# Moving eight row products and two table units of an expert layer ahead of its first pass

## The chip, the cores and the metric

The kernel runs on one core of a Trainium2 chip. Its engines are TensorE (matmuls), VectorE, ScalarE, GpSimd (here it mainly issues indirect DMAs) and SyncE (issues plain DMAs); 16 DMA engines move the data. The metric is the device time of one execution in microseconds (us), lower is better.

## The reference

One encoder block on 256 tokens of width 2048: two kinds of attention, an output projection, and then a product-key expert layer (PEER). The change touches only the last part:

```
qr = (h @ w_pq).reshape(b, t, 8, 2, 128)              # queries of 8 heads, two halves
sc = einsum(qr, sub_keys)                             # 128 scores per half
s_top, i_top = top_k(sc, 16)
cand = s_top[..., 0, :, None] + s_top[..., 1, None, :]
c_top, c_pos = top_k(cand, 16)                        # 16 picks per head
expert = i0 * 128 + i1                                # one of 16384 experts
g = softmax(c_top)
a = gelu(einsum(u_tab[expert], h))                    # 128 picks per token
out = einsum(g * a, v_tab[expert])
```

The tables `u_tab` and `v_tab` have 16384 rows of 2048 float32 numbers, 8 KB a row.

## The kernel before

The two halves of the tokens are treated in different ways, at the same time.

Tokens 128 to 255 are **dense**. TensorE reads each table in 128 units of 128 experts, 1 MB each. In the **first pass** (`u_chunk`) it multiplies unit after unit of `u_tab` with the tokens, 16 matmuls a unit; in the **second pass** (`v_chunk`) it multiplies the gated results with units of `v_tab`. Ring buffers hold the units: four in the first pass (`ring[0..3]`, two in the `raw` tile and two in `late`), six in the second. SyncE and ScalarE issue the loads of the first pass, each when the unit that held the buffer has been used. In the second pass GpSimd gathers the units from the seventh on, and leaves out the table rows of experts that no token uses.

Tokens 0 to 127 are **sparse**, one token per partition. For each of the 128 picks GpSimd gathers one table row per token (1 MB in all, an indirect DMA), and VectorE multiplies it with the token. The list `ROWS` has 256 of them: rows 0 to 127 are of `u_tab` ("u rows", one dot product each, `next_row`), rows 128 to 255 of `v_tab` ("v rows", added to the output in PSUM; rows whose weight is zero are not fetched). `BUF` tells in which of 8 buffers row r lands. Buffers 0 and 1 are free early. Buffers 2 to 5 are in the tile `late`, which holds the split activations and weights until the query projection ends. Buffers 6 and 7 lie over the scores and are used from row `R_MORE` on. GpSimd issues rows 0 to `ROWS_U` - 1, and after that one unit of `v_tab` and some rows in turn; `end` in that loop sets how many rows stand behind each unit. All waits of an engine are in program order, so a gather that waits for a buffer holds up everything behind it on GpSimd.

Ahead of the first pass stands the **query projection** (`wide_piece`, 64 pieces of `w_pq`, two to a loaded block). ScalarE makes the high part of a piece (`w_hi`), VectorE the low part (`w_lo`, `split_lo_half`, called by `weights_low`), and TensorE multiplies both. Four pieces can be in work (`NPART`), and four blocks can be loaded (`NRAW`); SyncE loads a block when the low parts of the block four earlier are made. VectorE puts the picks (`top_k`) of the first `N_AHEAD` heads between these low parts, and after the projection the picks of the rest, each with two rows:

```
for hp in range(N_AHEAD, NH):
    top_k(0, hp)
    row_numbers(hp)
    next_row(2)
for hp in range(NH):
    top_k(1, hp)
    next_row(2)
next_row(2)
```

I call one turn of these loops a **round**: there are 13 of them before. After them VectorE does four more rows, waits until ScalarE has taken the exponentials of the gates (`cexp_done`, in ScalarE's order behind the GELU of unit 60), and normalises the gates. Two rows later it copies the transposed picks (`slotT`), builds one-hot tables (`hots`), and from unit 64 on applies gates to the units (`gate`, `apply`), one row for each two units. `hs` is the normalised token that each u row is multiplied with; its gain vector lies in row buffer 1 until `hs` is made.

## Time and profile before

| what | value |
|---|---|
| median of 3 runs | 1543.37 us (1543.35 to 1543.79) |
| the profiled execution | 1542.8 us, span of its trace 1540.8 us |
| query projection, about | 408 to 508 us of the span |
| first pass (128 units of `u_tab`) | 509 to 1004 us |
| second pass (128 units of `v_tab`) | 1005 to 1538 us |
| busy share of the span | TensorE 95%, VectorE 75%, ScalarE 32%, GpSimd 28% |
| moved by DMA | 516 MB |
| granted TensorE clock, mean | 0.991 |

All times inside the kernel are read in us from the start of the span. The profile counts an engine as busy while an instruction runs on it, also while that instruction is held up inside. Of the DMA engines it gives the mean busy share and the rate.

### The profile page before, as it was taken

The page shows a single profiled execution, that of the slowest core. Times are in us where ns is not written, and L with a number is a line of the kernel's source. Part 1 is how long each engine was busy: PE and PEld are TensorE (multiplying, and loading weights), DVE is VectorE, ACT ScalarE, POOL GpSimd, SP SyncE. Part 2 cuts the span into 40 slices and gives each one's busy share as a digit, 9 for nine tenths or more (in the row PEclk, how much of TensorE's full clock was granted, in tenths as well). Part 3 has the DMA queues.
Part 4 walks back from the last instruction along what each step waited for, and adds up shares of the span by engine and source line. Part 5 has one row for each costly group of instructions (what it writes and reads, how often), then busy time and mean ns, then how long its engine had stood idle before and what let it go on. Part 6 is the DMA issues. An engine that isn't in the chain of part 4 may idle for free.

```text
span 1540.8 us, 21876 instructions
## 1 busy us (share of the span) xinstructions
PE 1457.5 (95%) x7977; PEld 1095.4 (71%) x7977; DVE 1155.3 (75%) x1797; ACT 488.4 (32%) x1402; POOL 429.7 (28%) x422
## 2 busy tenths in 40 slices
PE   8999999999999999999999999988778898999998
PEld 6767888888999999999999999943323333334333
DVE  5425688576777999992387777797766899999996
ACT  6647566765655100000254444472000000000000
POOL 2020000000000422230111111164454566666661
PEclk9999999999999999999999999999999999999999
DMA  9774544637574999999999999999999999999995
GB/s 352 264 138 122 161 124 137 218 124 255 196 253 168 375 422 421 422 421 422 418 421 422 422 410 405 419 413 417 419 418 418 406 390 390 405 405 384 399 402 225
DMA packets 115529, 516.24 MB, mean 335 GB/s; under 512 B 26113, under 2 KB 28289, under 8 KB 63313
## 3 DMA queue, kind: packets, MB, share of 16 engines
q0 software_dynamic: 57776, 294.93, 48.3%
q1 hardware_dynamic: 47744, 153.04, 27.7%
q10 hardware_dynamic: 9936, 67.40, 10.5%
q8 instruction: 34, 0.56, 0.1%
q14 instruction: 39, 0.31, 0.1%
HBM read 628.91 MB, written 3.41 MB: 410 GB/s over the span
## 4 chain that ended last, share of the span: by engine, by line
PE 51%; DMA 28%; DVE 12%; issue 4%; POOL 3%; ACT 1%; SPq 0%; POOLq 0%; DVEq 0%; ACTq 0%
PE ps L1572 18%; DMA late<-in_u_tab 11%; DVE ps L1183 9%; PE ps L1356 6%; PE ps L1361 6%; PE ps L1358 6%; DMA late<-in_v_tab,acts 6%; DMA raw<-in_v_tab,acts 3%; PE ps L1617 3%; DMA late<-in_u_rows,sel 3%; PE ps L1378 2%; PE ps L1520 2%; PE ps L1515 2%; PE ps L1516 2%; DMA raw<-in_u_tab 2%
## 5 line engine op out<-in xcount | busy, mean ns | idle before, releaser
L859 DVE TENSOR_TENSOR w_lo<-raw,w_hi 128x512 fp32r<-128x512 f32 (+1 forms) x288 | 188.8, 682 | 130.8 <-ACT w_hi L552 129.1
L1572 PE MATMUL ps<-acts,late 128*128 128x128 f32 x2048 | 240.4, 276 | 6.5 <-DMA late<-in_u_tab 5.7
L1572 PEld LDWEIGHTS ps<-acts,late 128*128 128x128 f32 x2048 | 233.1, 192 | 10.7 <-DMA late<-in_u_tab 7.8
L1572 PE MATMUL ps<-acts,raw 128*128 128x128 f32 x1984 | 232.2, 276 | 3.6 <-DMA raw<-in_u_tab 2.8
L1572 PEld LDWEIGHTS ps<-acts,raw 128*128 128x128 f32 x1984 | 225.8, 192 | 7.0 <-DMA raw<-in_u_tab 4.9
L552 ACT ACTIVATE w_hi<-raw 128x512 fp32r<-128x512 f32 (+1 forms) x288 | 170.1, 622 | 85.8 <-PE ps L1520 41.9
L1617 PE MATMUL ps<-raw,acts 128*128 128x512 f32 x352 | 163.0, 613 | 21.2 <-DMA raw<-in_v_tab,acts 19.8
L1617 PE MATMUL ps<-late,acts 128*128 128x512 f32 x336 | 155.6, 611 | 21.3 <-DMA late<-in_v_tab,acts 19.2
L1617 PE MATMUL ps<-acts 128*128 128x512 f32 x336 | 154.8, 609 | 22.0 <-DMA acts<-in_v_tab,acts 21.2
L508 POOL DMA_INDIRECT late<-in_u_rows,sel x70 | 85.8, 1225 | 271.4 <-DVE late L1174 260.7
L1183 DVE SCALAR_TENSOR_TENSOR ps<-late,sel,ps 128x2048 f32<-128x2048 f32 x63 | 148.3, 2355 | 12.2 <-DMA late<-in_v_tab,acts 5.2
L1183 DVE SCALAR_TENSOR_TENSOR ps<-acts,sel,ps 128x2048 f32<-128x2048 f32 x63 | 148.3, 2354 | 8.4 <-DMA acts<-in_v_tab,acts 1.8
L1356 PE MATMUL ps<-w_hi,hT_hi 128*128 128x512 f32 (+1 forms) x448 | 148.5, 412 | 2.9 <-DVE hT_lo L872 2.6
L1617 PEld LDWEIGHTS ps<-raw,acts 128*128 128x128 f32 x352 | 66.4, 194 | 115.3 <-issue 76.8
L508 POOL DMA_INDIRECT acts<-in_u_rows,sel x58 | 66.7, 1150 | 281.5 <-DVE acts L1174 178.1
L1617 PEld LDWEIGHTS ps<-late,acts 128*128 128x128 f32 x336 | 62.7, 193 | 112.9 <-issue 68.8
L1617 PEld LDWEIGHTS ps<-acts 128*128 128x128 f32 x336 | 63.1, 193 | 112.0 <-issue 71.6
L1361 PE MATMUL ps<-w_lo,hT_hi 128*128 128x512 f32 (+1 forms) x448 | 137.6, 388 | 0.6 <-DVE w_lo L859 0.6
L1358 PE MATMUL ps<-w_hi,hT_lo 128*128 128x512 f32 (+1 forms) x448 | 138.0, 389 | 0.0
L1356 PEld LDWEIGHTS ps<-w_hi,hT_hi 128*128 128x128 f32 x448 | 80.8, 189 | 24.0 <-issue 6.5
L1361 PEld LDWEIGHTS ps<-w_lo,hT_hi 128*128 128x128 f32 x448 | 84.4, 189 | 18.2 <-DVE w_lo L859 1.1
L1174 DVE SCALAR_TENSOR_TENSOR late<-late,acts 128x2048 f32<-128x2048 f32 x40 | 90.7, 2287 | 8.8 <-DMA late<-in_u_rows,sel 8.7
(225 smaller groups left out, 1938.4 us busy)
## 6 DMA issues: line engine op xcount, KB each, us to landing
raw<-in_w_in SPq DMA_DIRECT2D x72, 512.0 KB, 3.8
late<-in_u_tab SPq DMA_DIRECT2D x33, 1024.0 KB
raw<-in_u_tab SPq DMA_DIRECT2D x32, 1024.0 KB
late<-in_u_tab ACTq DMA_DIRECT2D x31, 1024.0 KB
raw<-in_u_tab ACTq DMA_DIRECT2D x30, 1024.0 KB
raw<-in_w_o SPq DMA_DIRECT2D x32, 512.0 KB, 3.7
raw<-in_w_pq SPq DMA_DIRECT2D x32, 512.0 KB, 3.5
raw<-in_w_in SPq DMA_DIRECT2D x8, 400.0 KB, 3.4
```

Source lines behind the costliest of these rows:

```text
L508: pool.indirect_dma_start(row[BUF[r]], None, io["u_rows"], bass.IndirectOffsetOnAxis(ap=idx[:, n:n + 1], axis=0)).then_inc(row_in[BUF[r]], 16)
L552: nc.scalar.activation(whi[(2 * j + half) % NPART][:, 0:w], raw[j % NRAW][:, half * w:half * w + w], ACT.Copy).then_inc(hi_done, 1)
L859: V.tensor_tensor(wlo[slot_no][:, 0:w], raw[j % NRAW][:, half * w:half * w + w], whi[slot_no][:, 0:w].bitcast(F32), ALU.subtract).then_inc ...
L1174: V.scalar_tensor_tensor(row[BUF[r]], row[BUF[r]], 1.0, held if moved else hs, ALU.mult, ALU.mult, accum_out=a_sel[:, n:n + 1]).then_inc(r ...
L1183: V.scalar_tensor_tensor(held, row[BUF[r]], w_sp[:, n:n + 1], acc if r == V_ROW[0] else held, ALU.mult, ALU.add).then_inc(row_used, 1)
L1356: mm(out[b], hT_hi[:, k, t[b]], whi[part][:, 0:w], start=start and kk == 0, stop=False)
L1358: mm(out[b], hT_lo[:, k, t[b]], whi[part][:, 0:w], start=False, stop=False)
L1361: ins = mm(out[b], hT_hi[:, k, t[b]], wlo[part][:, 0:w], start=False, stop=stop and kk == 1)
L1378: ins = mm(ps[:, bank, :], src[:, k, b * P:b * P + P], w[:, k, :], start=k == 0, stop=k == ks - 1)
L1515: mm(out, whi[piece % NPART][:, w], hT_hi[:, k, :], start=k == 0, stop=False)
L1572: ins = mm(ps[:, q, 0:N_DN], unit[:, k * P:k * P + P], hF[:, k, :], start=k == 0, stop=k == KD - 1)
L1617: ins = mm(out_bank(n), acts_c[i * V_FULL + q], ring[q][:, 512 * n:512 * n + 512], start=first, stop=last)
```

## The change

Six things are changed together.

- The picks of one head instead of three are made between the low parts of the query projection (`N_AHEAD`), so that there are 15 rounds behind it. `hs` is made right behind head 0's picks.
- Eight rows (`R_FRONT`) alternate between buffers 0 and 1 during the query projection: VectorE does one behind each four low parts, seven in all, and the eighth at the end. All are picks of head 0.
- Four units of `u_tab` instead of two go to places of their own (`first_units`), each behind a few blocks of `w_pq` on SyncE's queue, and the four ring buffers start with units 4 to 7. To make room, `x2[1]` and `subk` move in the tile `acts`.
- GpSimd's fill of ones over a part of `acts` now waits for the use of unit 3, since two first units lie under it; 14 gathers instead of 6 stand ahead of it.
- The first pass carries twelve rows more: `ROWS_U` goes from 76 to 88, and `ROWS_SB`, VectorE's count at its end, from 69 to 81. `R_MORE` and a table `BUF_FREE` follow the new buffers.
- The other rows are spread over all of the second pass's gathered units, and the last few stand behind the last unit.

```diff
@@ -173,17 +173,19 @@
-        x2 = [acc, region(A_WU, D)]
+        A_X2 = 5 * D
+        assert A_X2 >= TT * IN_W
+        x2 = [acc, region(A_X2, D)]
...
-        A_SUBK = A_WU + TT * D
+        A_SUBK = A_X2 + D
...
-        first_units = [region(2 * UNIT * i, 2 * UNIT) for i in range(2)]
+        first_units = [region(2 * UNIT * i, 2 * UNIT) for i in (0, 1, 4, 7)]
@@ -332,19 +334,21 @@
-        N_AHEAD = 3
+        N_AHEAD = 1
...
-        ROWS_U = 76
-        R_MORE = 40
-        BUF = [r % 6 for r in range(R_MORE)] + [(6, 7, 4, 5, 0, 1, 2, 3)[(r - R_MORE) % NROW] for r in range(R_MORE, 2 * N_PICK)]
+        ROWS_U = 88
+        R_FRONT, R_MORE, ROWS_PICKED = 8, 46, 39
+        BUF = [r % 2 for r in range(R_FRONT)] + [(2, 3, 4, 5, 0, 1)[(r - R_FRONT) % 6] for r in range(R_FRONT, R_MORE)]
+        BUF += [(6, 7, 4, 5, 0, 1, 2, 3)[(r - R_MORE) % NROW] for r in range(R_MORE, 2 * N_PICK)]
         BUF_TURN = [BUF[:r + 1].count(BUF[r]) for r in range(2 * N_PICK)]
+        BUF_FREE = [max((q + 1 for q in range(r) if BUF[q] == BUF[r]), default=0 if r < R_MORE else ROWS_PICKED) for r in range(2 * N_PICK)]
...
-        ROWS_SB = 69
+        ROWS_SB = 81
@@ -405,24 +409,31 @@
+            query_weights(0, 3)
             sp.wait_ge(piece_used, 2 * B_PQ + 2)
...
+            first_unit(0)
+            query_weights(3, 4)
+            first_unit(1)
+            query_weights(4, 5)
+            first_unit(2)
+            query_weights(5, 6)
+            first_unit(3)
+            query_weights(6, 8)
...
             for j in range(2, NRING):
-                sp.dma_start(ring[j], u_unit(j)).then_inc(unit_in[j], 16)
-            sp.wait_ge(unit_used, 3)
-            sp.dma_start(ring[2], u_unit(NRING + 2)).then_inc(unit_in[2], 16)
+                sp.dma_start(ring[j], u_unit(NRING + j)).then_inc(unit_in[j], 16)
@@ -514,11 +525,11 @@
-            gathers(0, 6)
-            pool.wait_ge(score_done, 2 * NH)
+            gathers(0, R_FRONT + 6)
+            pool.wait_ge(unit_used, NRING)
             pool.wait_ge(x2_stored, 16)
             pool.memset(region(A_ONES, NKEY * N_DN - A_ONES), 1.0).then_inc(ones_set, 1)
-            gathers(6, ROWS_U)
+            gathers(R_FRONT + 6, ROWS_U)
@@ -527,9 +538,10 @@
-                end = ROWS_U + (len(ROWS) - ROWS_U) * min(u + 1 - V_FULL, NKEY - 4 - V_FULL) // (NKEY - 4 - V_FULL)
+                end = ROWS_U + (len(ROWS) - ROWS_U) * (u + 1 - V_FULL) // (NKEY + 3 - V_FULL)
                 gathers(done, end)
                 done = end
+            gathers(done, len(ROWS))
@@ -1214,13 +1226,18 @@
             for hp in range(N_AHEAD):
                 top_k(0, hp, weights_low)
                 row_numbers(hp)
-                weights_low()
-                weights_low()
-            while lo_halves[0] < 2 * U_PQ:
-                weights_low()
+            weights_low()
+            weights_low()
             dve.wait_ge(gain_row_in, 16)
             V.scalar_tensor_tensor(hs, x2[0], rs_x[:, 0:1], row[1], ALU.mult, ALU.mult).then_inc(hs_ready, 1)
             dve.wait_ge(hs_ready, 1)
+            weights_low()
+            while lo_halves[0] < 2 * U_PQ:
+                for _ in range(4):
+                    weights_low()
+                if rows_done[0] < R_FRONT - 1:
+                    next_row()
+            next_row(R_FRONT - rows_done[0])
```

VectorE in the query projection, from the end of head 0's picks, before (`w_lo` is a low part, the second row makes the row numbers of the gathers):

```order
L1163 TENSOR_SCALAR acts<-acts 128x16
L1212 SCALAR_TENSOR_TENSOR sel<-acts 128x16
L859 TENSOR_TENSOR w_lo<-raw,w_hi 128x512 x2
L1128 COPY acts<-acts 128x256
L859 TENSOR_TENSOR w_lo<-raw,w_hi 128x512
L1130 MAX acts<-acts 128x8 x2
```

and in the change (L1232 makes `hs`, L1186 is a row product):

```order
L1175 TENSOR_SCALAR acts<-acts 128x16
L1224 SCALAR_TENSOR_TENSOR sel<-acts 128x16
L871 TENSOR_TENSOR w_lo<-raw,w_hi 128x512 x2
L1232 SCALAR_TENSOR_TENSOR acts<-acts,stat 128x2048
L871 TENSOR_TENSOR w_lo<-raw,w_hi 128x512 x5
L1186 SCALAR_TENSOR_TENSOR acts,sel<-acts 128x2048
L871 TENSOR_TENSOR w_lo<-raw,w_hi 128x512 x4
```

The short steps of two heads between single low parts have gone behind the projection, and instead of them an instruction on 2048 columns stands behind each four low parts.

GpSimd from its first gathers to those behind the fill, before:

```order
L508 DMA acts<-in_u_rows,sel 128x2048 [waits idx_ready]
L508 DMA acts<-in_u_rows,sel 128x2048 [waits hs_ready]
L508 DMA late<-in_u_rows,sel 128x2048 [waits piece_used]
L508 DMA late<-in_u_rows,sel 128x2048 x3
L520 MEMSET acts 128x8192 [waits x2_stored,score_done]
```

and in the change:

```order
L519 DMA acts<-in_u_rows,sel 128x2048 [waits idx_ready]
L519 DMA acts<-in_u_rows,sel 128x2048 [waits hs_ready]
L519 DMA acts<-in_u_rows,sel 128x2048 [waits row_used] x6
L519 DMA late<-in_u_rows,sel 128x2048 [waits piece_used]
L519 DMA late<-in_u_rows,sel 128x2048 x3
L519 DMA acts<-in_u_rows,sel 128x2048 [waits row_used] x2
L531 MEMSET acts 128x8192 [waits x2_stored,unit_used]
```

Six gathers that wait for a row product each now stand ahead of those that wait for the end of the projection (`piece_used`).

GpSimd at the end of the second pass, before (L528 gathers a unit, L510 a v row):

```order
L528 DMA late<-in_v_tab,acts 128x2048 [waits unit_used]
L510 DMA late<-in_v_tab,acts 128x2048 [waits row_used] x2
L528 DMA acts<-in_v_tab,acts 128x2048 [waits unit_used] x2
L528 DMA raw<-in_v_tab,acts 128x2048 [waits unit_used] x2
```

and in the change (L539 a unit, L521 a v row):

```order
L521 DMA late<-in_v_tab,acts 128x2048 [waits row_used]
L539 DMA raw<-in_v_tab,acts 128x2048 [waits unit_used]
L521 DMA acts<-in_v_tab,acts 128x2048 [waits row_used] x2
L521 DMA late<-in_v_tab,acts 128x2048 [waits row_used] x2
L521 DMA acts<-in_v_tab,acts 128x2048 [waits row_used] x2
```

The last four gathers were units, and are now rows: six of them stand behind the last unit.

## Rows read from the trace of the kernel before

**Rows 1.** The page's fourth part, the chain that ended last: share of each engine

```profile
PE 51%; DMA 28%; DVE 12%; issue 4%; POOL 3%; ACT 1%; SPq 0%; POOLq 0%; DVEq 0%; ACTq 0%
```

**Rows 2.** Busy time of each engine by stretch, with clock, DMA share, rate

```profile
core 0: us, PE busy (x) PEld busy (x) DVE busy (x) ACT busy (x) POOL busy (x), PEclk, DMA share, GB/s
450.00:505.00 55.00, 55.00 (x463) 55.00 (x463) 41.40 (x113) 27.37 (x52) 1.21 (x1) 1.00 0.56 188
505.00:690.00 185.00, 176.93 (x1525) 172.32 (x1524) 178.30 (x515) 15.75 (x51) 60.90 (x33) 1.00 1.01 419
690.00:750.00 60.00, 58.97 (x505) 57.27 (x504) 12.89 (x15) 7.42 (x19) 6.26 (x6) 1.00 1.01 422
...
900.00:1004.00 104.00, 103.82 (x924) 103.47 (x923) 78.62 (x113) 49.48 (x149) 13.68 (x14) 1.00 1.00 411
...
1510.00:1541.00 31.00, 25.45 (x59) 10.47 (x57) 18.35 (x14) 0.00 (x0) 1.98 (x2) 1.00 0.48 177
```

**Rows 3.** What the DMA engines moved in 508:1004, 1004:1176 and 1176:1541

```profile
DMA packets 28474, 207.54 MB, mean 418 GB/s; under 512 B 3146, under 2 KB 3146, under 8 KB 3146
...
DMA packets 12356, 71.66 MB, mean 417 GB/s; under 512 B 3516, under 2 KB 3516, under 8 KB 3644
...
DMA packets 33917, 138.81 MB, mean 380 GB/s; under 512 B 15930, under 2 KB 15930, under 8 KB 17338
```

**Rows 4.** By stretch, TensorE's matmuls of the second pass (L1617) alone

```profile
1004.00:1176.00 172.00, 138.44 (x283) 55.88 (x284) 0.93 1.02 417
1176.00:1510.00 334.00, 304.62 (x685) 125.86 (x684) 1.00 1.01 399
1300.00:1400.00 100.00, 93.95 (x214) 39.22 (x213) 1.00 1.01 403
```

**Rows 5.** A group of VectorE's v rows in 1300:1400: busy us, mean ns, idle before

```profile
L1183 DVE SCALAR_TENSOR_TENSOR ps<-late,sel,ps 128x2048 f32<-128x2048 f32 x20 | 47.1, 2355 | 2.9 <-DMA late<-in_v_tab,acts 0.7 <-DVE ps L1183 0.5
```

**Rows 6.** Timeline of VectorE and GpSimd, 451:521: start, us, instruction, [idle before]

```profile
451.07 0.18 DVE L1212 SCALAR_TENSOR_TENSOR sel<-acts 128x16 uint32<-128x16 f32 x1
451.52 1.21 POOL L508 DMA_INDIRECT acts<-in_u_rows,sel  x1 [41.73 <-DVE sel L1212]
...
475.88 0.18 DVE L1212 SCALAR_TENSOR_TENSOR sel<-acts 128x16 uint32<-128x16 f32 x1
475.98 0.68 DVE L859 TENSOR_TENSOR w_lo<-raw,w_hi 128x512 fp32r<-128x512 f32 x1
...
513.36 6.95 POOL L520 MEMSET acts<- 128x8192 f32 x1
513.98 6.37 DVE L1163 TENSOR_SCALAR acts<-acts 128x16 f32<-128x16 f32 x1
```

**Rows 7.** DMA issues in 451:462; the last number is the median us to landing

```profile
raw<-in_w_pq SPq DMA_DIRECT2D x3, 512.0 KB, 6.7
```

**Rows 8.** Timeline of VectorE, 668:757

```profile
668.42 2.29 DVE L1174 SCALAR_TENSOR_TENSOR late<-late,acts 128x2048 f32<-128x2048 f32 x1
...
681.84 2.29 DVE L1174 SCALAR_TENSOR_TENSOR acts<-acts 128x2048 f32<-128x2048 f32 x1
...
701.74 2.29 DVE L1174 SCALAR_TENSOR_TENSOR late<-late,acts 128x2048 f32<-128x2048 f32 x1 [5.16 <-DMA late<-in_u_rows,sel]
...
709.19 2.29 DVE L1174 SCALAR_TENSOR_TENSOR acts<-acts 128x2048 f32<-128x2048 f32 x1 [5.16 <-DMA acts<-in_u_rows,sel]
...
746.98 0.42 DVE L1271 TENSOR_REDUCE acts<-acts 128x16 f32<-128x256 f32 x1 [28.33 <-ACT acts L806]
...
756.57 0.56 DVE L1278 COPY slotT<-ps 128x384 f32<-128x384 f32 x1 [3.73 <-PE ps L1579]
```

**Rows 9.** Timeline of TensorE in the second pass: two places, and its end

```profile
1020.80 7.03 PE L1617 MATMUL ps<-acts 128*128 128x512 f32 x16
...
1248.96 7.13 PE L1617 MATMUL ps<-acts 128*128 128x512 f32 x16 [1.33 <-DMA acts<-in_v_tab,acts]
...
1523.45 7.13 PE L1617 MATMUL ps<-acts 128*128 128x512 f32 x16 [0.65 <-DMA acts<-in_v_tab,acts]
```

More of the change, by code:

```diff
@@ L246, in build_block @@
         unit_in = [sem(f"unit_in{i}") for i in range(V_FULL)]
-        first_in = [sem(f"first_in{i}") for i in range(2)]
+        first_in = [sem(f"first_in{i}") for i in range(NRING)]
         value_in = [sem(f"value_in{i}") for i in range(V_FULL)]
@@ L406, in u_unit, with query_weights, first_unit @@
                 return io["u_tab"][ds(v * P, P), :]
-            with sp.Fori(0, U_PQ // 8) as i:
-                for j in range(4):
-                    load(i * 4 + (B_PQ + j), j, io["w_pq"][ds(i * (4 * P) + j * P, P), :])
-            sp.wait_ge(piece_used, 2 * B_PQ + 2)
-            for j in range(2):
-                sp.dma_start(first_units[j], u_unit(j)).then_inc(first_in[j], 16)
-            with sp.Fori(U_PQ // 8, U_PQ // 4) as i:
-                for j in range(4):
-                    load(i * 4 + (B_PQ + j), j, io["w_pq"][ds(i * (4 * P) + j * P, P), :])
+            def query_weights(first, end):
+                with sp.Fori(first, end) as i:
+                    for j in range(4):
+                        load(i * 4 + (B_PQ + j), j, io["w_pq"][ds(i * (4 * P) + j * P, P), :])
+            def first_unit(j):
+                sp.dma_start(first_units[j], u_unit(j)).then_inc(first_in[j], 16)
+            query_weights(0, 3)
+            sp.wait_ge(piece_used, 2 * B_PQ + 2)
+            first_unit(0)
[6 more added lines that the diff above has]
+            query_weights(6, 8)
             for j in range(2):
@@ L498, in gather @@
                     pool.wait_ge(hs_ready, 1)
-                if r == 2:
+                if r == R_FRONT:
                     pool.wait_ge(piece_used, 2 * B_U)
@@ L504, in gather @@
                     pool.wait_ge(value_ready, n // TOPK + 1)
-                if r >= 6:
-                    pool.wait_ge(row_used, r + 1 - (6 if r < R_MORE else NROW))
+                if BUF_FREE[r]:
+                    pool.wait_ge(row_used, BUF_FREE[r])
                 if kind == "u":
@@ L801, in _ @@
                 gelu(c)
-                if c % 2 and c > 1:
+                if c % 2 and c > 3:
                     odd_unit(c + NRING)
@@ L1564, in u_chunk @@
                     pe.wait_ge(score_done, 2 * NH)
-                early_unit = isinstance(i, int) and i == 0 and q < 2
+                early_unit = isinstance(i, int) and i == 0
                 if early_unit:
@@ L1568, in u_chunk @@
                 else:
-                    pe.wait_ge(unit_in[q], i * 16 + (16 if q >= 2 else 0))
+                    pe.wait_ge(unit_in[q], i * 16)
                 unit = first_units[q] if early_unit else ring[q]
@@ L1612, in v_chunk @@
                 if isinstance(i, int) and i == 0:
-                    pe.wait_ge(unit_in[q], 16 * (NKEY // NRING + (1 if q >= 2 else 0)) if q < NRING else 16)
+                    pe.wait_ge(unit_in[q], 16 * (NKEY // NRING) if q < NRING else 16)
                 else:
```

## The prediction

> **What bounds the kernel now.** I read the chain that ended last first [rows 1]: half of it is TensorE, but 28% of the span is waiting for a DMA, so it is no plain compute bound. The stretches say where [rows 2]. In the query projection (450:505) TensorE is busy all the time and the DMA engines move 188 GB/s. From 505 on they move 419 to 422 GB/s with a busy share of 1.01, whatever the engines do, and this goes on to 1510. So the DMA engines are full for a thousand us and have more than half of their rate free in front of that. In the first pass TensorE still loses little: 8 of 185 us in 505:690, 1 of 60 in 690:750, 0.2 of 104 in 900:1004. There DMA and TensorE are both full, and the row transfers fill what the units leave over.
>
> What was moved [rows 3]: 207.5 MB in the first pass, 71.7 MB in 1004:1176, 138.8 MB from there to the end. TensorE's matmuls of the second pass [rows 4] are eight to a unit: 283 / 8 = 35.4 units in the first 172 us (4.9 us a unit), 685 / 8 = 85.6 in the next 334 (3.9 us a unit), the last 7 in the tail. The first stretch is slow because its rows are u rows, of which all 1.05 MB come; a v row or a gathered unit brings some 0.58 MB (210.5 MB of the second pass, less about 55 u rows, 3 plain units and 3 MB of residual and output, over 250 gathers). In 1300:1400 the pace is 26.75 units, 3.74 us each, and VectorE does a v row in 2.36 us with about 0.1 between two [rows 5], so 2.46. At 180 rows for 118 units, 1.525 each, that is 3.75 us a unit: in the steady part VectorE sets the pace, with TensorE 94% busy and the DMA engines at 403 GB/s close behind.
>
> **The change, part by part.** *Query projection.* VectorE's row numbers of heads 0 and 1 lie 24.8 us apart [rows 6], and 16 low parts go in that time: 6.2 us for four. It will do four low parts and a row, 4 x 0.7 + 2.3 = 5.1 us, so it has the time. One row holds the low parts up by 2.3 us; four pieces (some 1.55 us each) can be in work, so TensorE needs a low part at the earliest some 4 us after it can be made. No loss, while rows are there in time. A buffer is filled again while the other's row is waited for and used: 12.4 - 2.3 - 0.3 = 9.8 us for issue and landing. Row 0's gather was issued at 451.5 [rows 6]; beside it a `w_pq` load took 6.7 us to land [rows 7], and the gather, twice as large, is likely to take 8 to 9. The free rate holds them: a row in 6.2 us is 169 GB/s, on top of the 188, and two more units 40. That is 397 of 421. Cost 0, up to 4 us if rows come late. If the cover were gone, each us that a row is late is a us of TensorE's.
>
> A rule speaks against this. The Trainium skill (DMA: Bandwidth & Descriptors, "Queues, rings and completion order") has each DMA engine take the queues that have work in turn, packet by packet, so `w_pq` gets only its share beside a gather; the 6.7 us of [rows 7] agree. By it alone a load behind a 1 MB unit on SyncE's queue waits for 1.57 MB at half of 421 GB/s, 7.5 us. Block loads are issued four blocks of 3.1 us ahead, so the sum stays the same.
>
> *First pass.* VectorE starts its rounds at the same time as before, about 505: behind the last low part one instruction on 2048 columns is left, a row now and `hs` before. It has 15 rounds instead of 13. One takes 13.42 us [rows 8], so 27 us more. It has 28.3 us of idle time ahead of the gates at 746.98 and some 18 us of waits for rows before it. The fill of ones, now behind unit 3, runs at about 525 to 532. In [rows 6] an instruction on 16 columns took 6.37 us inside the fill; I let the same loss stand. New is that rows 8 and 9 are issued only at 508, with other gathers and units beside them; I give 4 us. So VectorE comes to the gates at about 746.98 - 28.33 + 27 + 4 = 749.5, 2 us late. Behind it two rows that used to lie ready are now waited for, at 7.46 us from row to row [rows 8]: `slotT` at about 764 instead of 756.6. ScalarE needs the one-hot tables near 764, so TensorE loses 2 to 5 us here. The transfers give the same: rows used in the pass rise by 5 (81 - 8 against 69 - 1), units loaded in it fall by 2: 3 x 1.05 = 3.1 MB more. The pass had 1.1 MB to spare in 900:1004 (411 against 422 GB/s), so 2 MB / 0.421 = 5 us. Saved is about 1 us of waits for units 2 and 3. I take +5 for the pass, bounds -1 and +12 (all of VectorE's lateness and the waits behind it).
>
> The Trainium skill (SBUF — State Buffer, "SBUF: two separate sides") calls the port pair of VectorE and GpSimd an exclusive lock, taken for a whole instruction against VectorE's instructions in a two-port mode, or with two inputs if GpSimd reads. By it a fill that reads nothing would let a row product pass: if the new place falls on one, up to 2.3 us of the 6.4 are saved. That changes VectorE's arrival, hardly the sum.
>
> *Second pass, u rows.* VectorE has 187 rows left before and 175 after; the twelve are u rows. 12 x 1.05 = 12.6 MB. And u rows end sooner: 40 gathers at 168 / 125 = 1.344 a unit instead of 52 at 1.525, so about unit 36 instead of 40: 4 units (2.5 MB) less lie in the stretch. 71.66 - 12.6 - 2.5 = 56.6 MB at 417 GB/s is 136 us instead of 172: **-36**. It carries 35.4 - 4.3 = 31.1 units.
>
> *Second pass, v rows.* 96.9 units are left, in the trace 92.6 in 362 us (1176 to 1538). The spread lowers the rows to 1.344 a unit: VectorE 1.344 x 2.46 = 3.31 us a unit. DMA: 138.8 + 2.5 - 2.1 (outputs) = 139.2 MB at 403 GB/s, 345 us, or 3.56 a unit. TensorE: two units in 7.03 us where they lie ready, 7.24 with the gap between where each is waited for [rows 9], so 3.52 to 3.62. All three stand within 8%, so they will get in each other's way. I take 3.68, between TensorE's 3.62 and the 3.74 of [rows 4]: 357 us, **-5**. Bounds: 3.52 (341 us, -21) and 3.90 as now (378 us, +16). In the tail the DMA engines ran at 177 GB/s [rows 2], TensorE doing its last four units alone from 1523 [rows 9]; with rows behind the last unit that is filled. It is inside the -5. Six rows behind the last gather are 15 us of VectorE against 21 us of TensorE for its six buffers, so neither ends far behind.
>
> *Sum.* Against the profiled span: 0 + 5 - 36 - 5 = -36, span 1504.8. The median stands 2.6 us above that span (1543.37 against 1540.8): **1507 us**.
>
> **Rivals.**
> - *VectorE bounds the first pass.* Rows come at 7.46 us and a pair of units takes 7.65, so a lateness of 7 us hardly shrinks up to unit 127 and ScalarE and TensorE take it over, with 5 us more for late rows: +15 for the pass instead of +5, 1517. For it: VectorE is busy 178 of 185 us in 505:690. Against: the idle 28 us, and TensorE's stalls give the DMA engines time.
> - *The last stretch keeps its pace.* DMA and not VectorE sets it, at 3.8 or 3.9 us a unit: 96.9 x 3.82 = 370, +8 instead of -5: 1520. For it: share 1.01 throughout. Against: VectorE's v rows stand back to back in 1300:1400, with landed data.
> - *The last stretch runs at TensorE's own pace*, 3.52: 1491.
> - *Slower than before: rows late in the projection.* VectorE waits in order, low parts and `w_pq` loads behind the row. Landing and issue in L us make a pair of rows take L + 2.6 us instead of 12.4, 3.5 pairs, less the slack of 4. It eats the gain of 36 us when 3.5 (L - 9.8) = 40, at L = 21; at 24 us it costs 46, and the time is 1553. For it: in the full first pass a row lands each 7.46 us, so with two ahead of it on the queue one takes 22. Against: here only one other row is on its queue, and the engines are half free.
> - *It does nothing.* The rows taken from the second pass come back as stalls of the first, 12.6 MB at 421 GB/s, +30 more there: 1540 or so. Against: only 3.1 MB are added to the pass; the rest goes in front of it.
>
> **How the numbers follow.** Forecast 0.50 (1500 to 1514), VectorE in the first pass 0.18, kept pace 0.15, TensorE's pace 0.10, nothing 0.03, slower 0.04. The range for 8 in 10 leaves out half of the fast case and the last two and holds the two slower-than-forecast cases: 1494 to 1524. A measurement of this kernel can tell about 0.2%, 3 us. Faster 0.93, same 0.03, slower 0.04.
>
> **What the new profile would show.** Right: DMA near 390 GB/s in 450:505 and TensorE still 55 of 55; the first row of the projection used at about 460; VectorE's idle time before the gates gone; the first pass over between 1003 and 1012; the u rows over near 1145; then 3.6 to 3.75 us a unit, TensorE and not VectorE in the chain, and a DMA tail of under 20 us. Wrong: low parts that wait behind a row for a DMA; TensorE idle for more than 15 us between 700 and 1000; or 3.8 us and more a unit behind 1150, with VectorE idle for DMA.

## The result, and the profile after

The change makes the kernel faster by 1.2%: 1524.3 us median (1523.74 to 1527.39, 4 runs) against 1543.58 (1543.35 to 1544.21, 4 runs), ratio 0.9879 [0.9861, 0.9896]. That is a gain of 19 us where 36 were forecast, and just outside the range of 1494 to 1524. The profiled execution, the slowest of the four, took 1527.39 us with a span of 1525.4. Of all the executions reported here one, of the run with less work for TensorE, took 2052.17 us at a granted clock of 0.656, where the others of that run had 0.984 to 0.987; it is left out of that run's numbers.

The page of the changed kernel: its first line, the packets and bytes, and the chain that ended last (before: [rows 1]). Here and below, `...` stands for rows or lines left out.

```profile
span 1525.4 us, 21815 instructions
...
DMA packets 115527, 516.23 MB, mean 338 GB/s; under 512 B 26112, under 2 KB 28288, under 8 KB 63312
...
PE 49%; DMA 26%; DVE 18%; issue 3%; ACT 1%; POOL 1%; another core or an unknown queue 0%; DVEq 0%; POOLq 0%; ACTq 0%; SPq 0%
```

The bytes are the same as before. Waits for DMA hold 26% of the chain instead of 28%, and VectorE 18% instead of 12%. By stretch, with the columns of [rows 2], and first one row of the kernel before:

```profile
505.00:560.00 55.00, 52.39 (x456) 51.27 (x455) 52.98 (x153) 6.59 (x18) 23.24 (x12) 1.00 1.01 413
```

```profile
450.00:505.00 55.00, 54.13 (x450) 53.52 (x449) 40.31 (x54) 26.69 (x53) 9.38 (x8) 1.00 0.89 337
505.00:560.00 55.00, 52.81 (x462) 52.25 (x461) 49.00 (x137) 6.42 (x18) 21.34 (x13) 1.00 0.96 387
...
690.00:750.00 60.00, 57.67 (x503) 56.60 (x501) 39.72 (x92) 6.37 (x18) 18.57 (x13) 1.00 1.01 422
750.00:900.00 150.00, 142.93 (x1244) 141.41 (x1243) 109.22 (x151) 64.85 (x193) 19.71 (x20) 0.99 1.01 421
900.00:1004.00 104.00, 103.78 (x919) 103.35 (x918) 78.36 (x115) 51.26 (x154) 13.04 (x13) 1.00 1.01 420
```

In the projection the DMA engines moved 337 GB/s instead of 188. But in 505:560 they moved 387, where the kernel before moved 413. In 900:1004 the rate is 420 instead of 411 in this profile: the slack of the pass has been used up. In the run again, below, it was 412, so this differs from execution to execution.

The first gates, on VectorE (start, us, instruction, [idle time before]). Before, they were reached at 746.98 after 28.33 us of idle time, and `slotT` at 756.57 [rows 8].

```profile
755.62 0.41 DVE L1288 TENSOR_REDUCE acts<-acts 128x16 f32<-128x256 f32 x1
...
760.56 2.29 DVE L1186 SCALAR_TENSOR_TENSOR late<-late,acts 128x2048 f32<-128x2048 f32 x1 [3.52 <-DMA late<-in_u_rows,sel]
...
767.71 2.29 DVE L1186 SCALAR_TENSOR_TENSOR late<-late,acts 128x2048 f32<-128x2048 f32 x1 [4.85 <-DMA late<-in_u_rows,sel]
...
769.93 0.55 DVE L1295 COPY slotT<-ps 128x384 f32<-128x384 f32 x1
```

And what that costs TensorE, in its own timeline:

```profile
775.07 1.22 PE L1605 MATMUL ps<-hot_a 128*128 128x256 f32 x4 [4.61 <-ACT hot_a L789]
```

The second pass: two rows of TensorE's matmuls alone (L1634 is L1617 of before; compare [rows 4]) and one of all engines, for 1500:1510. Behind them the last matmuls and VectorE's last work, and then the last matmuls and the last add of the kernel before:

```profile
1015.00:1180.00 165.00, 137.39 (x291) 55.86 (x292) 0.96 1.02 417
1180.00:1510.00 330.00, 319.34 (x734) 137.62 (x732) 1.00 0.98 385
...
1500.00:1510.00 10.00, 6.95 (x17) 2.78 (x15) 9.58 (x5) 0.00 (x0) 0.99 (x1) 1.00 0.50 189
```

```profile
1499.92 7.03 PE L1634 MATMUL ps<-raw,acts 128*128 128x512 f32 x16
```

```profile
1487.62 2.36 DVE L1195 SCALAR_TENSOR_TENSOR ps<-acts,sel,ps 128x2048 f32<-128x2048 f32 x1 [1.36 <-DMA acts<-in_v_tab,acts]
...
1514.67 2.35 DVE L1195 SCALAR_TENSOR_TENSOR ps<-acts,sel,ps 128x2048 f32<-128x2048 f32 x1
1517.13 2.72 DVE L1193 SCALAR_TENSOR_TENSOR acts<-acts,sel,ps 128x512 f32<-128x512 f32 x4
1519.77 2.48 DVE L1344 TENSOR_TENSOR acts<-ps,acts 128x512 f32<-128x512 f32 x4
```

```profile
1530.42 7.03 PE L1617 MATMUL ps<-raw,acts 128*128 128x512 f32 x16
...
1537.49 0.69 DVE L1327 TENSOR_TENSOR acts<-ps,acts 128x512 f32<-128x512 f32 x1 [0.17 <-PE ps L1617]
```

TensorE's last matmul ends at 1506.95. Before, it ended at 1537.45, and all that was left then was a last add of VectorE, 0.7 us. Now VectorE works alone for 15 us, one row each 2.46 us. The DMA engines are half idle in 1500:1510 (share 0.85 up to 1505 and 0.16 behind it), so I take it that the last data lands near 1505, and that the rows behind that were in their buffers.

The whole difference by stretches, from the timelines of both executions:

| us | before | after | difference | forecast |
|---|---|---|---|---|
| start to the first unit's matmul | 509.4 | 511.9 | +2.6 | 0 |
| first pass, first unit to first matmul of the second pass | 495.8 | 503.7 | +7.9 | +5 |
| second pass to VectorE's first v row | 199.0 | 164.6 | -34.4 | -36 |
| from there to the last add | 334.0 | 342.0 | +8.0 | -5 |
| sum | | | -15.9 | -36 |

The split of the second pass at the first v row isn't the prediction's: that one took 1176 us as the end of the u rows. The sum of the two parts does not depend on it: 533.0 us before, 506.6 after, so -26.4 where -41 were forecast. In bytes, the DMA engines moved 8.8 MB more ahead of the first unit (107.5 against 98.8), 3.5 MB more in the first pass (211.0 against 207.5) and 12.2 MB less in the second pass (197.7 against 210.0).

### The profile page after: what moved, and what is told of

Read it like the earlier page. It is cut to its first block, busy times and chain, and to the rows that moved or that the text cites. A ratio compares the mean times of both kernels' runs of the same rounds, so it can differ in the third digit from the quotient of the medians.

```text
span 1525.4 us, 21815 instructions
## 1 busy us (share of the span) xinstructions
PE 1448.7 (95%) x7977; PEld 1099.6 (72%) x7977; DVE 1153.4 (76%) x1797; ACT 486.7 (32%) x1402; POOL 428.1 (28%) x422
## 2 busy tenths in 40 slices
DMA packets 115527, 516.23 MB, mean 338 GB/s; under 512 B 26112, under 2 KB 28288, under 8 KB 63312
## 3 DMA queue, kind: packets, MB, share of 16 engines
q10 hardware_dynamic: 9792, 66.35, 10.5%
## 4 chain that ended last, share of the span: by engine, by line
PE 49%; DMA 26%; DVE 18%; issue 3%; ACT 1%; POOL 1%; another core or an unknown queue 0%; DVEq 0%; POOLq 0%; ACTq 0%; SPq 0%
PE ps L1589 12%; PE ps L1634 10%; DMA acts<-in_v_tab,acts 9%; PE ps L1373 6%; PE ps L1378 6%; PE ps L1375 6%; DMA late<-in_u_rows,sel 5%; DVE ps L1195 3%; DMA late<-in_v_tab,acts 3%; DVE late L1186 3%; DMA late<-in_u_tab 2%; PE ps L1395 2%; DVE acts L1186 2%; DMA raw<-in_w_pq 2%; DMA acts<-in_u_rows,sel 2%
## 5 line engine op out<-in xcount | busy, mean ns | idle before, releaser
L1589 PE MATMUL ps<-acts,late 128*128 128x128 f32 x1984 | 233.9, 277 | 9.0 <-DMA late<-in_u_tab 7.2
L1589 PEld LDWEIGHTS ps<-acts,late 128*128 128x128 f32 x1984 | 227.1, 193 | 13.1 <-ACT acts L777 6.6
L1634 PE MATMUL ps<-raw,acts 128*128 128x512 f32 x352 | 163.2, 617 | 18.8 <-DMA raw<-in_v_tab,acts 17.5
L1195 DVE SCALAR_TENSOR_TENSOR ps<-acts,sel,ps 128x2048 f32<-128x2048 f32 x63 | 148.3, 2355 | 20.1 <-DMA acts<-in_v_tab,acts 13.8
L1195 DVE SCALAR_TENSOR_TENSOR ps<-late,sel,ps 128x2048 f32<-128x2048 f32 x63 | 148.3, 2355 | 17.6 <-DMA late<-in_v_tab,acts 10.4
L1634 PE MATMUL ps<-late,acts 128*128 128x512 f32 x336 | 150.9, 598 | 10.2 <-DMA late<-in_v_tab,acts 9.5
L1634 PE MATMUL ps<-acts 128*128 128x512 f32 x336 | 150.2, 597 | 5.7 <-DMA acts<-in_v_tab,acts 4.9
L1634 PEld LDWEIGHTS ps<-raw,acts 128*128 128x128 f32 x352 | 68.2, 197 | 110.9 <-issue 82.6
L519 POOL DMA_INDIRECT acts<-in_u_rows,sel x62 | 72.9, 1175 | 264.2 <-DVE acts L1186 211.7
L519 POOL DMA_INDIRECT late<-in_u_rows,sel x66 | 78.9, 1196 | 233.4 <-DVE late L1186 212.8
L1634 PEld LDWEIGHTS ps<-late,acts 128*128 128x128 f32 x336 | 62.6, 190 | 95.9 <-issue 72.0
L1634 PEld LDWEIGHTS ps<-acts 128*128 128x128 f32 x336 | 62.7, 190 | 90.6 <-issue 72.5
L1186 DVE SCALAR_TENSOR_TENSOR late<-late,acts 128x2048 f32<-128x2048 f32 x43 | 97.7, 2287 | 25.1 <-DMA late<-in_u_rows,sel 24.9
```

The lines of the kernel that those rows point to most:

```text
L519: pool.indirect_dma_start(row[BUF[r]], None, io["u_rows"], bass.IndirectOffsetOnAxis(ap=idx[:, n:n + 1], axis=0)).then_inc(row_in[BUF[r]], 16)
L1186: V.scalar_tensor_tensor(row[BUF[r]], row[BUF[r]], 1.0, held if moved else hs, ALU.mult, ALU.mult, accum_out=a_sel[:, n:n + 1]).then_inc(r ...
L1195: V.scalar_tensor_tensor(held, row[BUF[r]], w_sp[:, n:n + 1], acc if r == V_ROW[0] else held, ALU.mult, ALU.add).then_inc(row_used, 1)
L1589: ins = mm(ps[:, q, 0:N_DN], unit[:, k * P:k * P + P], hF[:, k, :], start=k == 0, stop=k == KD - 1)
L1634: ins = mm(out_bank(n), acts_c[i * V_FULL + q], ring[q][:, 512 * n:512 * n + 512], start=first, stop=last)
```

## The experiments

Two readings stood against each other. **Bytes**: from 505 us on the DMA engines are full whatever the engines do, so only bytes that pass in front of that count. **Pace**: an engine's own speed (VectorE at the gates and in the v rows, TensorE in its units, one engine alone at the end) sets a stretch, and shortening its work shortens the kernel. Each group below shared a chip and the runs of the kernel before.

### Again, the end rule, and the rows around the gates

The first group had the kernel before at 1543.83 us. The changed kernel again:

> The changed kernel once more, beside the next three on one chip. Both theories: 1524 us, ratio 0.987 to 0.989.

1523.52 us, ratio 0.9863 [0.9847, 0.988].

The change with the old end rule:

```diff
-                end = ROWS_U + (len(ROWS) - ROWS_U) * (u + 1 - V_FULL) // (NKEY + 3 - V_FULL)
+                end = ROWS_U + (len(ROWS) - ROWS_U) * min(u + 1 - V_FULL, NKEY - 4 - V_FULL) // (NKEY - 4 - V_FULL)
```

> The change with the old rule for the end: all rows stand ahead of the last four units, 1.424 a unit instead of 1.344. Theory 'lag of VectorE at the end': with six rows behind the last unit and up to eight more in the buffers VectorE has 14 rows x 2.46 = 34 us left when TensorE has six units, 21 us; so the old rule takes 10 to 15 us off the changed kernel, 1510 to 1514, and both engines end within 5 us. Rival 'all three are full': rows that come sooner delay units by the same bytes, TensorE's pace falls from 3.5 to 3.6 us a unit and more, and the time stays at 1520 to 1526.

1525.39 us, 0.9878 [0.9862, 0.9895]: the 10 to 15 us of the first theory are not there, and the time is the rival's. TensorE now ends last, at 1519.1 instead of 1503.5, while VectorE ended its rows at 1507.9 and then waited. The 15 us in which VectorE works alone are gone and nothing is won. In this run's timeline VectorE waits 8.67 us for TensorE:

```profile
1505.20 2.72 DVE L1193 SCALAR_TENSOR_TENSOR acts<-acts,sel,ps 128x512 f32<-128x512 f32 x4
1516.60 1.48 DVE L1344 TENSOR_TENSOR acts<-ps,acts 128x512 f32<-128x512 f32 x2 [8.67 <-PE ps L1634]
```

The kernel before with only the new end rule:

> The kernel before with only the new rule for the end (1.44 rows a unit instead of 1.525, six rows behind the last unit). Lag theory: TensorE ends some 15 to 20 us sooner, since 1.44 x 2.46 = 3.54 us a unit replace 3.75, but VectorE's last 14 rows add 13 us: 1536 to 1542, at best a small gain. Rival 'the rows moved into the projection brought all of the gain, the spread none': 1543 and no change in TensorE's pace.

1544.51 us, 0.9999 [0.999, 1.0009], above the 1536 to 1542 expected; the rival's total, but not its unchanged pace of TensorE. Alone it is worth nothing: TensorE's part of the second pass is 14.5 us shorter (517.7 against 532.2), the tail behind it 13.4 us longer.

The change with the four rows that stand before and behind the gates moved to the end of the first pass:

```diff
-            next_row(4)
+            next_row(2)
             dve.wait_ge(cexp_done, 1)
...
-            next_row(2)
             dve.wait_ge(slotT_mm, 1)
...
-            next_row(3)
+            next_row(7)
             assert rows_done[0] == ROWS_SB
```

> The changed kernel with four of the rows that stand around the gates (two ahead of them, two ahead of the copy of slotT) done at the end of the first pass instead. Theory 'VectorE is late at the gates': slotT is copied near 759 instead of 770, TensorE's 4.6 us of waiting for the one-hot tables near 770 is gone, and the first pass takes 497 to 500 us instead of 504; time 1517 to 1521. Rival 'bytes': the pass carries 3 transfers more than before over full DMA engines, so the same us come back as waits for units: pass 503 to 505, time 1523 to 1526.

1524.33 us, 0.9874 [0.9857, 0.989]. TensorE's stall behind the gates is gone, as its timeline shows (compare 775.07 above), and the first pass is back at 495.6 us, 8.8 us less than in the run again. The second pass is 8.3 us longer. So VectorE's lateness does set the first pass, as forecast, but its price is no price of the kernel's. Each theory had one half of this: the total is that of bytes, the length of the pass that of VectorE's lateness.

```profile
767.02 0.72 PE L1604 MATMUL ps<-hot_a 128*128 128x256 f32 x4
767.58 3.74 PE L1588 MATMUL ps<-acts,late 128*128 128x128 f32 x32
```

### Taking work from one resource at a time

The second group (before: 1543.95 us) takes some 20 us of work in the last stretch from the DMA engines, from VectorE and from TensorE in turn, each on top of the change. `LESS` is `range(154, 246, 12)`, eight v rows. The changed kernel itself did not run in this group; its gain of 20.3 us is that of the first group.

Less for the DMA engines:

```diff
-                if kind == "u":
+                if r in LESS:
+                    pool.dma_start(row[BUF[r]][:, 0:16], io["iota"][:, 0:16]).then_inc(row_in[BUF[r]], 16)
+                elif kind == "u":
```

> The changed kernel without the data of eight of the picked value rows: every twelfth gather from number 154 to 238 is replaced by a copy of 16 columns, so 8 x 1.05 = 8.4 MB less pass the DMA engines in the last stretch, while VectorE and TensorE do all their work (eight products read what the buffer held before, so the output is not the reference's). Theory that the DMA engines' bytes set the end (the sum is bytes over a full set of engines): 8.4 MB by 0.40 MB per us is 21 us less, 1501 to 1506. Rival, TensorE's own pace of 3.4 to 3.5 us a unit sets it, and the DMA share of 1.00 is only packets that wait: under 5 us less, 1518 to 1523. Rival, VectorE's 2.46 us a row sets it: also under 5 us less.

1512.12 us, 0.979 [0.9774, 0.9807]: 31.8 us less than before, 11.5 more than the changed kernel's 20.3. The page shows that I had the edit's size wrong: a row that has weight zero is left out of its gather, so eight gathers were 516.23 - 510.95 = 5.28 MB and not 8.4.

```profile
DMA packets 114631, 510.95 MB, mean 338 GB/s; under 512 B 25740, under 2 KB 28044, under 8 KB 63068
```

5.28 MB at the 392 GB/s that the run again moved in 1180:1500 are 13.5 us. With its size corrected in this way, behind the result, the theory of bytes meets the 11.5 us within 2; the two of pace (under 5 us) do not. The edit takes eight indirect gathers from GpSimd too, some 1.3 us each, and no run tried GpSimd by itself. Against it as the limit: in 1200:1500 of the run again it waited some 60 us for TensorE and VectorE to free buffers, and a gather landed 15.7 us (median) behind its issue, so that it was well ahead of the data.

Less for VectorE:

```diff
-                        if r == V_ROW[1]:
+                        if r in LESS:
+                            V.scalar_tensor_tensor(held[:, 0:16], row[BUF[r]][:, 0:16], w_sp[:, n:n + 1], held[:, 0:16], ALU.mult, ALU.add).then_inc(row_used, 1)
+                        elif r == V_ROW[1]:
```

> The changed kernel with the products of the same eight value rows cut to 16 of 2048 columns on VectorE (the output leaves out the rest of these eight rows): 8 x 2.36 = 19 us of VectorE less, all bytes and all matmuls kept. Theory of bytes: 1520 to 1523, at most the tail behind TensorE's last matmul shrinks by a few us. If VectorE's row pace sets the end: up to 19 us less, 1504.

1525.44 us, 0.9878 [0.9862, 0.9895]. VectorE has 19 us less to do and the kernel is no faster (18.5 us less than before, against 20.3; the intervals overlap).

Less for TensorE:

```diff
-                for n in range(KD // 4):
+                for n in range(1 if isinstance(i, int) and i * V_FULL + q in range(60, 124, 8) else KD // 4):
```

> The changed kernel with eight units of the second table (60, 68, to 116) multiplied over the first 512 of 2048 columns only (the output leaves out the rest of these): 8 x 0.75 x 3.4 = 20 us of TensorE less, all bytes and all rows kept. Theory of bytes: 1518 to 1523. If TensorE's own pace sets the end: 1503 to 1508.

1525.25 us (three executions), 0.9873 [0.9853, 0.9893]. The same of TensorE: 20 us less, nothing won. In 1300:1400 it is busy 90.07 us instead of the 96.92 of the changed kernel, and the DMA engines' share is 0.98:

```profile
1300.00:1400.00 100.00, 90.07 (x199) 37.72 (x198) 86.53 (x38) 0.00 (x0) 62.40 (x64) 0.97 0.98 382
```

The fourth of the group puts the end rule between the two tried, with the last row's gather behind the last unit's:

```diff
-                end = ROWS_U + (len(ROWS) - ROWS_U) * (u + 1 - V_FULL) // (NKEY + 3 - V_FULL)
+                end = ROWS_U + (len(ROWS) - ROWS_U) * (u + 1 - V_FULL) // (NKEY - V_FULL)
```

> The changed kernel with an end rule between the old and the new one: the last row's gather is issued with the last unit's. In both rules tried the DMA engines are full to about 1500 and then one engine drains its buffers alone: VectorE for 17 us with TensorE idle, or TensorE for 19 us with VectorE idle. Theory that the end is full DMA engines until 1500 plus the longer drain: the backlog is shared, both end near 1512, total 1515 to 1519. Rival: the last landing moves too and nothing is won, 1521 to 1525.

1520.99 us, 0.9852 [0.9836, 0.9869], between the two expectations. TensorE ends at 1509.6 and VectorE's rows at 1512.2, so the backlog is shared. The DMA engines are nearly full in 1490:1500 here as well:

```profile
1490.00:1500.00 10.00, 9.42 (x22) 3.71 (x21) 8.43 (x5) 0.00 (x0) 3.30 (x4) 1.00 0.99 402
1500.00:1510.00 10.00, 9.28 (x21) 3.55 (x20) 9.58 (x5) 0.00 (x0) 0.00 (x0) 1.00 0.20 82
1510.00:1520.00 10.00, 0.00 (x0) 0.00 (x0) 4.62 (x8) 0.00 (x0) 0.00 (x0) 0.65 0.56 210
```

Its interval overlaps that of the change itself, so the 3 us stand on this only together with the last experiment.

### The dose, and the middle end rule elsewhere

The third group (before: 1544.34 us). Two heads picked ahead and four rows instead of eight (`N_AHEAD = 2`, `R_FRONT = 4`, `ROWS_U = 82`, `ROWS_SB = 75`, `R_MORE = 40`, `ROWS_PICKED = 33`):

> The changed kernel with half of the dose of rows: two heads picked ahead of the first pass, four row products there instead of eight, everything else as in the change. Theory of bytes (eight rows less made the second pass pay 11 to 21 us in the run that left out the gathers): four gathers, 4.2 MB, come back behind 505 us, 4.2 / 0.41 = 10 us, less the 1 to 2 us by which the first pass starts earlier: 1531 to 1535. Rival, the gain came from the units and the end alone: 1522 to 1526.

1532.97 us, 0.9926 [0.991, 0.9943]: 11.4 us faster than before, where the full dose is 20. This is the range of the theory of bytes; units and end alone, the rival, would have kept all of it.

The third and fourth unit behind the query weights:

```diff
-            first_unit(2)
-            query_weights(5, 6)
-            first_unit(3)
-            query_weights(6, 8)
+            query_weights(5, 8)
...
+            first_unit(2)
+            first_unit(3)
             sp.wait_ge(piece_used, 2 * B_U)
```

> The changed kernel with the third and fourth unit of the first table loaded behind the last of the query weights (as in the kernel before) instead of among them; all eight rows kept ahead. Theory of bytes: 2.1 MB come back behind 505 us, 5 us, less some of the 2.5 us that the query weights waited: 1525 to 1529. Rival, units are hidden either way: 1522 to 1524.

1524.76 us, 0.9873 [0.9857, 0.989]. Hardly slower, and between the two expectations: a little below what I expected from bytes. The windows say why. First this run, then the changed kernel again:

```profile
450.00:505.00 55.00, 55.00 (x464) 55.00 (x463) 43.45 (x56) 27.50 (x53) 9.38 (x8) 1.00 0.86 316
505.00:560.00 55.00, 53.65 (x472) 52.95 (x471) 45.94 (x131) 6.58 (x18) 20.98 (x13) 1.00 1.01 420
```

```profile
450.00:505.00 55.00, 55.00 (x464) 55.00 (x463) 43.21 (x55) 27.37 (x52) 9.38 (x8) 1.00 0.92 352
505.00:560.00 55.00, 53.58 (x473) 53.13 (x473) 49.22 (x147) 6.58 (x18) 21.48 (x13) 1.00 0.96 394
```

The two units move 36 GB/s x 55 us = 2.0 MB ahead of 505, but behind 505 the loads that follow wait for their buffers (SyncE 45.6 us of 505:560, for TensorE), and 26 GB/s x 55 us = 1.4 MB that the other run moves go unused. What the two units bring is 0.6 MB, 1.5 us; the gains over the kernel before differ by 0.7 us (20.3 and 19.6).

The middle end rule and the late rows together, on top of the change:

> The changed kernel with the middle end rule and with the four rows around the gates moved to the end of the first pass. Theory of bytes: the first pass is 8 us shorter and the second 8 us longer, total as with the middle end rule alone, 1519 to 1522. Rival, both gains add: 1512 to 1515.

1521.62 us, 0.9856 [0.9839, 0.9872]: the late rows add nothing to the middle end rule, as bytes have it.

And the middle end rule by itself, on the kernel before:

> The kernel before with the middle end rule alone. Theory: the end rule shares the last backlog between TensorE and VectorE and is worth the same 3 us here as on top of the change, 1540 to 1542; with the DMA engines as the limit until 1510 to 1520 and nothing moved ahead it can't be more. Rival: before has nothing to share, since VectorE ends its rows just ahead of TensorE, and it stays at 1543 to 1545.

1539.4 us, 0.997 [0.9958, 0.9983]. Alone on the kernel before, the middle rule is worth 4.9 us, more than the 3 expected: TensorE ends at 1527.4 instead of 1537.5, VectorE's rows at 1530.4. The rival of "nothing to share" falls. The last landing lies near 1515 to 1520, and behind it one engine drained its buffers alone in both of the other rules.

### All runs by one rule

The answer on the DMA engines for 0:560, before and for the run again:

```profile
DMA packets 43745, 119.95 MB, mean 214 GB/s; under 512 B 3835, under 2 KB 6011, under 8 KB 39499
```

```profile
DMA packets 44882, 128.21 MB, mean 229 GB/s; under 512 B 3964, under 2 KB 6140, under 8 KB 39628
```

In 560:1500 both kernels move 410 to 411 GB/s. So the gain should be the bytes moved by 560 beyond those of before, plus bytes left out, over 0.41 MB per us. The line is drawn at 560 because the rates of the two kernels still differ in 505:560. Measured is the median of before less that of the run, from the same chip; the bytes are those of the run's one profiled execution.

| run | MB by 560 us | more than before | over 0.41, us | measured, us |
|---|---|---|---|---|
| changed kernel, first result | 126.87 | 6.92 | 16.9 | 19.3 |
| again | 128.21 | 8.26 | 20.1 | 20.3 |
| old end rule | 127.60 | 7.65 | 18.7 | 18.4 |
| late rows | 128.12 | 8.17 | 19.9 | 19.5 |
| VectorE less | 127.82 | 7.87 | 19.2 | 18.5 |
| TensorE less | 127.51 | 7.56 | 18.4 | 18.7 |
| two units late | 127.51 | 7.56 | 18.4 | 19.6 |
| four rows | 123.98 | 4.03 | 9.8 | 11.4 |
| DMA less | 128.01 | 8.06 + 5.28 | 32.5 | 31.8 |
| new end alone | 118.99 | -0.96 | -2.3 | -0.7 |
| middle end | 128.20 | 8.25 | 20.1 | 23.0 |
| middle end, late rows | 128.12 | 8.17 | 19.9 | 22.7 |
| middle end on before | 119.95 | 0.00 | 0.0 | 4.9 |

Ten of thirteen lie within 2.4 us. The other three are those with the middle end rule, 2.8 to 4.9 us above the line. Part of the rest is scatter between executions: the code of the new end alone is that of before up to 560, and its profile has 1 MB less there. The sum was made behind the runs, and it does not test the rate: it shows that what counts is how much passes ahead, and that the end rule adds a few us of its own.

## Why the prediction was half right

- *What bounds the kernel.* The first reading, DMA engines full from 505 on with free rate in front, was the right one, and with the bytes that were in fact moved ahead of 560 it gives the result. The ten transfers that the change puts there, 10.5 MB, would be 26 us; 6.9 to 8.3 MB were left of them by 560, since in 505:560 the loads waited for free buffers and the DMA engines moved 387 to 394 GB/s instead of 413. The second, "in the steady part VectorE sets the pace", was wrong where it was tried: with 19 us less of VectorE's work the changed kernel keeps its time. Back-to-back rows on VectorE showed that it was busy, not that it was the limit. No run took work from VectorE in the kernel before, of which the reading was made.
- *Query projection, 0.* Nearly right. DMA engines at 337 to 352 GB/s against 397 forecast. `w_pq` loads took a median of 10.4 us to land in 450:505, and 8.0 in the run again (6.7 in [rows 7]), and ScalarE waited 14.7 us for them in eight waits in the first profile, 4.2 us in the run again. TensorE was busy 54.13 of 55 us in the first, 55.00 in the second. The first unit starts at 511.9 in the first profile but 509.9 in the run again, and at 511.8 in a run whose code is that of before up to there: of the +2.6 most is scatter. TensorE hardly felt it. The Trainium skill (DMA: Bandwidth & Descriptors, "Queues, rings and completion order") has the queues take turns, and the landings came later with more of them at work; the prediction's estimate of 7.5 us from it is near the 8.0 of one profile and below the 10.4 of the other.
- *First pass, +5.* Mechanism right, size +7.9. VectorE came to the gates at 755.6 and not at 749.5, and to `slotT` at 769.9 and not at 764; TensorE's stall was the 4.61 us forecast as 2 to 5. But the term is void in the sum: the run with late rows takes 8.8 us off the pass and gets 8.3 back behind it.
- *The fill of ones.* It held VectorE again: a cast of 32 columns and a product of 256 behind it took 4.99 and 4.90 us inside the fill (6.37 us in [rows 6]). No row product fell into it in this trace. In the run with two units late one did, but for its first 0.19 us: it took its usual 2.29 us and the fill its usual 6.93, and only the copy of 256 columns behind it was held, 5.05 us. That agrees with the rule of the Trainium skill (SBUF — State Buffer, "SBUF: two separate sides") on what a fill that reads nothing lets pass.

```profile
524.41 2.29 DVE L1185 SCALAR_TENSOR_TENSOR late<-late,acts 128x2048 f32<-128x2048 f32 x1 [2.37 <-DMA late<-in_u_rows,sel]
524.60 6.93 POOL L530 MEMSET acts<- 128x8192 f32 x1 [8.37 <-PE ps L1588]
526.62 5.05 DVE L1139 COPY acts<-acts 128x256 f32<-128x256 f32 x1
```

- *Second pass, u rows, -36.* Measured -34.4, over another stretch. VectorE was still in u rows until 1204 in the kernel before, where I had let them end at 1176, 35.4 units into the pass, although my own count put their end at unit 40. In the trace they end at unit 41 before and 36.5 after, the 4 units less of the forecast, so the size holds. In bytes the whole stretch goes from 82.84 MB (1005:1204) to 68.84 MB (1015:1180), 14.0 / 0.417 = 34 us.
- *Second pass, v rows, -5.* **This is the step that failed: +8.0.** The term, 357 us, took an engine's pace, TensorE's 3.68 us a unit, for the pace of the stretch and put nothing behind it ("neither ends far behind"). TensorE's pace came out as forecast: 98 units in the last 355 us of its work, 3.63 each, and 491.3 us for the whole second pass where 136 and 357 are 493. But behind its last matmul VectorE worked on alone for 15.3 us, and that is the size of the miss in this pass (14.6). The six rows behind the last gather were right; the "21 us of TensorE for its six buffers" beside them were not: TensorE ended 2 us behind the last data. Nor would another order of the last gathers have given the forecast. With the old end rule VectorE does not lag, and TensorE needs 506.2 us for the pass, 15 us more. The runs show the limit under both: bytes at the rate of the DMA engines, to which the prediction gave 345 us, at the 403 GB/s of one 100-us window. They moved 391 GB/s (125.1 MB in 1180:1500), which for the same 139.2 MB is 356 us, and 17 us of draining follow the last data near 1505: 373 us by this rough sum, 16 more than the term, where the second pass missed by 14.6. The end rule that was to remove the tail moved it from TensorE to VectorE, worth -0.7 us alone and within the measurement on top of the change.
- *The signs.* The first row product came at 462 (460 forecast), the idle time ahead of the gates was gone, and TensorE had 3.6 us a unit behind 1150, all as forecast. The u rows ended at 1180, not 1145, and the first pass at 1015.6, not by 1012. VectorE waited 27 us for the DMA engines in 1180:1500 of the run again (6 us in 1204:1500 before), one half of a sign of being wrong, and the chain ends in VectorE's work, not in TensorE's.
- *The sum.* It added stretches that share one full resource. What a stretch gave up was in part taken by the next. Counted once, in bytes ahead of 560 us, the change was worth 17 to 20 us. The start (+2.6 for 0), the first pass (+7.9 for +5) and the second (-26.4 for -41) are the 20 us between the two sums.
- *The rivals.* "The last stretch keeps its pace", 1520, came nearest: its reason, the DMA engines and not VectorE set it, is what the runs showed, with the first pass's extra 3 us and the start's on top. Its number is in part luck: it had 3.82 us a unit and no tail, and the trace has 3.63 and a tail of 15. "TensorE's own pace" fell with the run that took TensorE's work away, and so did "VectorE bounds the first pass" as a price of the whole.

The fastest version is the change with the middle end rule, 1520.99 us; with the late rows as well it is 1521.62, which is the same within the noise.

**Open:** why the DMA engines move less in the changed kernel's v rows, 115.7 MB in 1204:1500 against 117.6 before, with the same part of short packets (49%). The traces show where: in 1380:1410 their busy share is 0.96 at 350 GB/s (0.93 and 338 in the run again), where the kernel before has 1.00 and 399. These 30 us hold 1.5 of the 1.9 MB, and all runs with the change show the dip, 314 to 363 GB/s. In the run again a gather there landed 14 us behind its issue, against 16 in the 80 us ahead of it, which points to fewer gathers waiting in the queue; what empties it at this place no run tested.

## What to carry to other kernels

- Where one resource is full through several stages, don't sum gains by stage. Count what passes it in all, and what the edit moves to a time when it is free; then check that the free place behind the edit is still used, since work fetched early can leave the queue with nothing to fetch.
- An engine back to back with work is not shown to be the limit. Take a known amount of work from each resource in turn: here 19 us of VectorE and 20 us of TensorE were worth nothing, and 13 us of DMA were worth 11.
- At the end of a stream, what the buffers hold when the last transfer lands must still be worked off. Order the last transfers so that the engines end together: here 5 us on the kernel before.

## What was not expected of the hardware

- The DMA rate is lower where more of the gathered rows are left out, at nearly the same busy share: 391 to 398 GB/s with 49% short packets, 417 in 1015:1180 with 31% (3851 of 12347). In 1210:1300, away from the dip, both kernels have 393 to 394.
- A gather of 128 v rows moved 0.66 MB (5.28 MB for eight), less than the 1.05 MB of a full one. The prediction had 0.58 MB for such a row; the expectation of the run overlooked it.
